# Products of constants on TensorE ahead of the second block's norms

## The reference

```python
def second_block(x, ...):
    for l in range(DEPTH):                                   # DEPTH = 2
        h = swiglu_ffn(rmsnorm(x, ffn1_pre_g[l]), ffn1_w_gu[l], ffn1_w_down[l])
        x = x + 0.5 * rmsnorm(h, ffn1_post_g[l])
        h = mixing_sublayer(rmsnorm(x, mix_pre_g[l]), w_in[l], ...)
        x = x + rmsnorm(h, mix_post_g[l])
        h = swiglu_ffn(rmsnorm(x, ffn2_pre_g[l]), ffn2_w_gu[l], ffn2_w_down[l])
        x = x + 0.5 * rmsnorm(h, ffn2_post_g[l])
    return x
```

## Time and profile before

| | |
|---|---|
| median of 3 runs | 2138.0 us (2136.16 to 2138.79) |
| the profiled execution, its own time | 2139.36 us |
| its span, first to last instruction | 2137.7 us |
| mean granted TensorE clock | 0.964 |
| TensorE matmuls busy | 1985.0 us, 93% |
| VectorE, ScalarE, GpSimd busy | 58%, 43%, 11% |
| idle time of TensorE before the transposes of line 288 | 75.7 us at 6 places |

### The profile page before, as it was taken

How to read it: one execution, slowest core, us unless ns; L and a number is a source line. 1 busy time by engine, 2 the same in 40 slices (tenths; PEclk the granted TensorE clock), 3 DMA queues, 4 the chain that set the end, 5 groups by cost and what they waited for, 6 DMA issues and landing times.

```text
span 2137.7 us, 34658 instructions
## 1 busy us (share of the span) xinstructions
PE 1985.0 (93%) x13760; PEld 1859.0 (87%) x13760; DVE 1248.1 (58%) x1487; ACT 924.8 (43%) x955; POOL 240.7 (11%) x181
## 2 busy tenths in 40 slices
PE   7989999998999997999799979996999799988996
PEld 6989899888989996999699869996999699878996
DVE  6665655568566555454668574545444559565444
ACT  5454444445444444433434444344434434434342
POOL 0000000000000001000077040000000057150000
PEclk9989999998999998999899999998999999999998
DMA  7534555454345554555334445453555334444553
GB/s 270 181 120 141 190 182 187 154 176 153 118 176 207 186 187 148 191 180 182 123 131 149 156 150 202 179 182 128 191 179 191 114 139 159 155 160 175 180 191 113
DMA packets 50658, 356.83 MB, mean 167 GB/s; under 512 B 5968, under 2 KB 6128, under 8 KB 8432
## 3 DMA queue, kind: packets, MB, share of 16 engines
q1 hardware_dynamic: 47904, 344.06, 45.5%
q0 software_dynamic: 2640, 11.18, 1.6%
HBM read 353.12 MB, written 2.10 MB: 166 GB/s over the span
## 4 chain that ended last, share of the span: by engine, by line
PE 41%; issue 9%; DVE 6%; POOL 3%; ACT 1%; DVEq 0%; POOLq 0%; ACTq 0%
PE ps L183 13%; PE ps L184 13%; PE ps L185 13%; DVE w_lo L159 1%; DVE conv_y L1738 1%; POOL RL L1432 1%; PE ps L288 1%; DVE pss L129 1%; POOL GU L1434 1%; POOL GU L1432 1%; DVE b_gates L1666 0%; DVE score L1786 0%; DVE top L1781 0%; POOL RL L1434 0%; POOL sum L1410 0%
## 5 line engine op out<-in xcount | busy, mean ns | idle before, releaser
L159 DVE TENSOR_TENSOR w_lo<-raw,w_hi 128x2048 fp32r<-128x2048 f32 x325 | 758.9, 2338 | 497.1 <-ACT w_hi L152 496.6
L152 ACT ACTIVATE w_hi<-raw 128x2048 fp32r<-128x2048 f32 x326 | 622.9, 1913 | 442.6 <-PE ps L185 442.6
L183 PE MATMUL ps<-aH,w_hi 128*128 128x256 f32 x2752 | 787.6, 286 | 18.6 <-DVE w_lo L159 13.0
L184 PE MATMUL ps<-aL,w_hi 128*128 128x256 f32 x2752 | 783.2, 285 | 0.0
L185 PE MATMUL ps<-aH,w_lo 128*128 128x256 f32 x2752 | 782.8, 284 | 0.0
L183 PEld LDWEIGHTS ps<-aH,w_hi 128*128 128x128 f32 x2752 | 533.2, 194 | 25.8 <-issue 18.8
L184 PEld LDWEIGHTS ps<-aL,w_hi 128*128 128x128 f32 x2752 | 533.0, 194 | 2.4
L185 PEld LDWEIGHTS ps<-aH,w_lo 128*128 128x128 f32 x2752 | 532.6, 194 | 0.0
L183 PE MATMUL ps<-w_hi,mixH 128*128 128x512 f32 x768 | 299.8, 390 | 1.0 <-DVE mixL L392 1.0
L184 PE MATMUL ps<-w_lo,mixH 128*128 128x512 f32 x768 | 299.6, 390 | 0.0
L185 PE MATMUL ps<-w_hi,mixL 128*128 128x512 f32 x768 | 298.8, 389 | 0.0
(11 more groups left out here) (332 smaller groups left out, 1608.9 us busy)
## 6 DMA issues: line engine op xcount, KB each, us to landing
raw<-in_w_b SPq DMA_DIRECT2D x200, 1024.0 KB, 4.8
raw<-in_w_a SPq DMA_DIRECT2D x126, 1024.0 KB, 4.8
rows<-in_post_gains POOLq DMA_DIRECT2D x7, 512.0 KB, 4.1
rows<-in_rows_a POOLq DMA_DIRECT2D x2, 1028.0 KB, 6.4
rows<-in_par_b POOLq DMA_DIRECT2D x3, 385.0 KB, 3.4
x<-in_x SPq DMA_DIRECT2D x2, 512.0 KB, 6.5
bias_line<-a_gates POOLq DMA_DIRECT2D x1, 1024.0 KB, 13.0
out<-x SPq DMA_DIRECT2D x2, 512.0 KB, 3.6
```

The lines of the kernel that those rows point to most:

```text
L152: act.activation(k.w_hi[:, s, :], k.raw[:, s, :], ACT.Copy).then_inc(k.hi_ready, 1)
L159: dve.tensor_tensor(k.w_lo[:, s, :], k.raw[:, s, :], k.w_hi[:, s, :].bitcast(F32), ALU.subtract).then_inc(k.lo_ready, 1)
L183: pe.matmul(out, a[0], b[0], start=first, stop=False)
L184: pe.matmul(out, a[0], b[1], start=False, stop=False)
```

## The change

TensorE's program gets `keep_busy(n)`, which issues n plain products of the identity with the first 512 columns of `consts` in float32, each with start and stop set, all into PSUM bank 3. Nobody waits for them or reads them, and they wait for nothing. They stand in each of the two layers ahead of the three norms: 14, 12 and 9 of them. Since TensorE takes its instructions in order, the transposes stand behind them.

```diff
+            def keep_busy(n):
+
+                for _ in range(n):
+                    pe.matmul(k.ps[:, 3, :], k.ident, consts[:, 0:512], start=True, stop=True)
+
             with pe.Fori(0, DEPTH) as l:
+                keep_busy(14)
                 norm_transpose(k, pe, l, 0)
                 mlp(l, 0)
+                keep_busy(12)
                 norm_transpose(k, pe, l, 1)
                 for half in range(2):
...
                 t_last(k, pe, [(WO + i, lambda kt, i=i: aop(2 * i + kt)) for i in (2, 3)], t_out)
+                keep_busy(9)
                 norm_transpose(k, pe, l, 2)
                 mlp(l, 1)
```

## The result

The changed kernel takes 2147.19 us in the median of 5 runs (2146.77 to 2151.32) against 2138.79 us in the same session: a ratio of 1.0046, 95% interval 1.0031 to 1.006. A second session gave 2148.21 against 2138.30, ratio 1.0049 (1.0035 to 1.0062). It is slower by 0.46%, where 0.2% was forecast; the range ended at 2145.6. The profiled execution took 2146.77 us.

What follows compares the result with a forecast made beforehand. TensorE was taken to bound the kernel, its matmuls busy for 93% of the span. The terms, 6.0 - 0.4 - 0.2 - 0.8 = plus 4.6 us, on the median of 2138.0 gave 2142.6 us, range 2139.8 to 2145.6.

Steps and rivals of the forecast that it cites:

- The cost of a product: Each added product of 512 columns takes 0.86 us at the upper clock, as two records; 1.72 at the lower.
- Layer 0, norm 0: At the second block's entry the 14 products don't fit; the transposes wait 7.6 us: plus 6.0 us, bounds 5.3 and 6.5.
- Layer 1, norm 0: 14 products leave 4.3 us idle; the clock falls once more but returns sooner: minus 0.4 us, bounds minus 1.0 and plus 0.9.
- Norm 1 and the mixing layer behind it: Norm 1, both layers: 2.2 us left idle, clock stays up, nearly nothing to win: minus 0.1 us each, bounds 0 and minus 1.2.
- Norm 2: Both layers: 9 products leave 2.3 us idle and the clock stays up: minus 0.4 us each, other bound 0.
- The one that said the clock falls after the products all the same: Rival: transposes don't hold the clock after the products, all gains go; plus 6.0 us alone, 2144.0 us; chance 0.12.
- The one that had the runs before lose more than the profile: Rival: at norm 1 the clock returns late in other executions before; two layers give minus 2, 2140.6 us; chance 0.18.
- The short products: Rival: products are one record, 0.43 us, and fit at layer 0's first norm; other norms win nothing; 2138.0 us; chance 0.07.

Runs made afterwards that it cites:

- e3: Changed kernel with the 14 products moved from the head to the end of the loop's body: 2139.10 us, ratio 1.0003.
- e4: Changed kernel with 18, 14 and 11 products at the norms and 4 at the entry, filling the idle stretches: 2137.53 us, ratio 1.0002.
- e6: Changed kernel with the 14 and the 9 products taken out, only norm 1's 12 left: 2139.13 us, ratio 1.0006.
- e7: Kernel before with one filling of an unused tile on VectorE ahead of its first instruction of the second block: 2137.79 us, ratio 1.0.
- e2: Changed kernel with the 14 products taken out, only the 12 and the 9 left: 2139.84 us, ratio 1.0005.
- e12: Changed kernel with 2 more products behind norm 1's transposes: 2144.89 us, ratio 1.0036.
- e13: Changed kernel with 2 products behind norm 1's transposes, and 14 and 11 at norms 1 and 2 for 12 and 9: 2142.83 us, ratio 1.0021.
- e5: The changed kernel as it is, run once more: 2148.21 us; the second profile is of its fastest execution, 2141.4 us.
- e1: Changed kernel with the 12 and the 9 products taken out, only the 14 at the loop's head left: 2142.28 us, ratio 1.0019.

## Why the prediction was wrong

*The cost of a product, right.* 0.86 us was taken; 12 products took 10.46 us from the first start to the last end, the last record overlapping, so 0.86 each, as two records.

*Layer 0, norm 0, right.* The wait was forecast as 14.3 us of products and 7.6 us of lateness; measured are 14.29 (824.88 to 839.17) and 7.59 by the stretches. That 1.6 us come back through the faster transposes and first products also holds: 203.70 became 202.11. Plus 6.0 forecast, 6.0 in one profile and 6.2 in the other.

*Layer 1, norm 0: the size was off.* 4.3 us were to be left idle; it was 2.09. The first product came 1.79 us late, with "issue" as the reason. I take this for TensorE's jump back to the loop's head, which in the kernel before lay hidden in the wait: with the products at the end of the body (e3), ahead of the jump, they start without a gap and the rest is 4.30. With 2.09 left, the clock stayed up, and the MLP took 0.89 us less (minus 0.4 forecast, minus 1.0 the bound).

*Norm 1 and the mixing layer behind it: this step failed.* "12 products are 10.3 us of 12.46, leaving 2.2, less than any idle stretch after which the clock fell: it stays up." The shortest of four idle stretches, 2.6 us, is no bound. At norm 1 of layer 1 the clock fell 0.6 us behind the first transpose, after 2.17 idle. "VectorE's evictions follow its chunk split without a pause, so that faster transposes don't bring them forward" was right, and I drew only half of its consequence: the time that the transposes win becomes a pause of 2 us (1.97 against 0.48 before), and in e4's profile the clock came down at that pause, just as the mixing layer's products began. The upper bound of this term was 0. Measured by the stretches to norm 2 it is plus 0.4, plus 4.3 and, in the second profile, plus 0.6 and minus 2.2. And the norm is the smaller part of the 4.3: 1.66 us are lost there, 2.66 at the waits of feature chunks 16 and 24, 118 and 178 us on. The sum had no term for the clock there at all; it took what lies behind a norm's first chunk to be the same before and after, and the clock's falls in it are not.

*Norm 2: half right.* Minus 0.4 each was forecast, minus 0.5 and minus 0.1 measured. The second is read to the program's end. But the clock didn't stay up. It fell at 1283.28, 0.3 us behind the first transpose, and was back at 1286.7, before the second half of the first chunk:

```profile
1283.00:1284.00 1.00, 1.00 (x7) 0.64 0.00 0
1285.00:1286.00 1.00, 1.00 (x7) 0.50 0.00 0
1286.00:1287.00 1.00, 1.00 (x7) 0.66 0.41 82
```

*The rivals.* The one that said the clock falls after the products all the same was right in its place and wrong in its price: it gave up the gains and had no loss. It also added 3.4 us of transposes to the rest; at the upper clock they take 1.97. The one that had the runs before lose more than the profile is refuted in its price: taking products to norm 1 alone (e6) wins nothing, where it had minus 2. The late return that it supposed does occur: in e7's profile the clock came back 5.7 us behind layer 0's first transpose at norm 1, yet the mixing layer was no longer for it, 240.47 us. The short products are refuted by the two records. The Trainium skill, page "TensorE: Matmul & The Clock Gate", section on the PE-mode transpose, says that transposes don't count as TensorE activity in the same way, so that the full clock doesn't engage for them. That fits no better than before: in the changed kernel the clock stayed at 1.00 through norm 1 of layer 0,

```profile
1041.00:1045.00 4.00, 1.97 (x16) 1.00 0.11 16
```

with 2.16 us idle, 1.97 of transposes and 1.97 idle, 6 us without a product; had the transposes not counted, this would be longer than each of the four stretches, up to 5.3 us, after which the clock fell. e2, e3 and e6 show the same at both layers' norm 1. No run was made for it.

*What stays open.* The sum of the parts, 4.1 and 1.6 us by the medians, is less than the whole, 8.4 to 9.9. The mixing layer takes between 237.8 and 245.7 us in the profiles of the kernels that keep its small products in a row, by where the clock's falls come in it and how long they last, and that differs between executions of one kernel. That the changed kernel meets the long form more often than its parts do is what the times suggest; no profile counts it. Why a beginning 6 us later and the kept clock should do this together wasn't settled, nor why the same 2.17 us idle ahead of norm 1's transposes left the clock up in six places (e2, e3 and e6) and not in layer 1 of the changed kernel. e12 and e13 show only that filling the pauses takes up to half of the loss away.

## What to carry to other kernels

Filler on an engine that takes its work in order must be over before the real work is due, in every trip of a loop: count the time from the engine's entry, at the clock that it has there, and not from the idle stretch of a later trip. Where the clock is kept up only in part, its fall can come at a later place that holds more work; look at what the faster step will wait for next, and at the waits further on (here of 3.1 and 2.3 us), and either cover those pauses too or leave the filler out. Before filling gaps, look for stretches in which the engine is busy and yet at its lower clock: here a reordering of small products, without any filler, won 7.5 us, where filling all gaps at the norms and the pause behind one won 2.3. Add the ups and downs of the clock over the whole layer, not only at the place of the edit.

## What the runs showed that I had not expected

- A clock fall on a busy engine: 48 products of 4 columns in a row, then 10.2 us at 1.2 GHz in each layer of the kernel before; set singly between products of 256 columns, none.
- The length of one and the same instruction stream differs by 6.55 us of some 240 between two executions of one kernel, and the granted clock accounts for it.
- At the loop's head TensorE's first instruction of layer 1 came 1.6 to 1.8 us late in three profiles (change, e5, e1), invisible while a wait covers it; that this is the jump is argued from its place.
- More than half of a loss of 4.3 us lay over 100 us behind the edit, at two waits that the edit doesn't touch.
- With the clock at 1.00 through the second block, the spread was 0.8 us in 5 runs, against 2.7 in 15 before: this points to the clock as the source of most of this kernel's scatter, and was not tested further.
